# Channel LayerNorm of a convolution branch: cross-partition sums by a matrix of ones against transposes with tokens on partitions, with a weight split moved into the same stage

## The chip, the cores and the metric

The kernel runs on one core of a Trainium2 chip. The metric is the time of one execution on the device in microseconds (us); lower is better. Kernels are compared by the median of several runs.

## The reference

Two request groups (512 and 1024 tokens, width 1024) go through a two-layer encoder with the same weights. In the kernel they are one array of 1536 rows (12 tiles of 128 tokens). The part that matters here is layer 0's mixer:

```python
def conv_branch(u, gate, w, b, g, beta):
    h = u * jax.nn.sigmoid(gate)
    h = depthwise_conv_width_31(h, w) + b            # per channel, along the tokens
    return jax.nn.silu(layer_norm(h, g, beta))       # mean and variance over the 512 channels

conv_out = conv_branch(u, gate, conv_w, conv_b, cln_g, cln_b)
attn_out = window_attention(q, k, v, sink)
mix = jnp.concatenate([conv_out, attn_out], axis=-1) @ w_out     # 1024 -> 1024
x = layer_norm(ALPHA * x + mix, ln1_g[layer], ln1_b[layer])      # then the router and the experts
```

`layer_norm` subtracts the mean over the channels, multiplies by 1/sqrt(variance + 1e-5), then by a gain and adds a shift per channel. All is float32. The products with `w_out` are made of three passes on numbers rounded for the fast matmul path: high x high, high x low, low x high, where low is what high leaves of the number.

## The kernel before, in words

`trunk` calls one function per stage. Every stage opens with `Core.stage()`: it takes its own buffers and semaphores, holds one block of instruction streams (one per engine, in written order), and ends with a barrier of all engines (L129). So work of different stages never overlaps, and what one stage ends later starts all that follow later.

The stages around the change, in layer 0:

`window_and_taps` (its last instructions end at 503 us of the span) leaves the convolution's result in `cat[:, 0:4, :]`: channels on partitions (4 tiles of 128 channels), 1536 tokens along the row. `cat[:, 4:8, :]` holds the attention's output in the same layout. During it SP also loads the raw output weights, 8 pieces `early[k]` of 128 x 1024.

`norm_channels` (L639) normalises over channels, which here lie across partitions. It works in three chunks of 512 tokens. PE multiplies a 128 x 128 matrix of 1/512 with the 4 channel tiles (L685): each partition of `mean_ps` then holds the mean of each token. DVE subtracts it in place (L672), ACT squares 4 x 512 columns (L713), PE sums the squares in the same manner (L694), ACT takes the root (L715), DVE the reciprocal of 512 columns (L676) and multiplies (L679), ACT applies gain, shift and Silu from per-partition columns (L720). All three chunks of reciprocals and products stand behind the three subtractions in DVE's order.

`project_out` (L774) multiplies `cat` by the output weights, tile by tile of 128 tokens. It first splits the weights: ACT copies `early[k]` into `wh` (L991), DVE subtracts to get `wl` (L942), and PE waits for `w_low` piece by piece during tile 0's first half (`arriving`, L861 and following). Of each token tile ACT makes `ah` (L954), DVE `al` (L910), PE runs 48 matmuls of 512 columns (L864), DVE adds the residual (L917) and normalises the row (L162 to L173, with 1/sqrt by POOL's `pow`, L851), PE transposes it (L887) for the router. `ah`, `al` have two slots, `y_ps` two halves of PSUM.

`experts` and layer 1 follow, with barriers between them; `project_out` also serves layer 1, where 5 of 8 weight pieces are loaded in its own stage.

Of the kernel before, what the change touches and what calls it, by code (L numbers as in the profile page):

```python
# [14 lines left out]
P = 128  # L15
D = 1024
KD = D // P
# [621 lines left out]
def norm_channels(c, m, acc, cat):  # L639
    nc = c.nc  # L640
    with c.stage():
        par = c.sb("conv_par", [P, 2, CT])
        ones = c.sb("ones", [P, P])
        eps = c.sb("eps", [P, 1])
        sq = c.sb("sq", [P, 2, CT, HALF])
        rstd = c.sb("rstd", [P, TOK // HALF, HALF])
        mean_ps, var_ps = c.ps("mean_ps", TOK), c.ps("var_ps", HALF)
        loaded, dve, const = c.sem("loaded"), c.sem("dve"), c.sem("const")
        mean_done, centred, squared, var_done, rooted, normed, cat_done = (
            c.sem(n) for n in ("mean_done", "centred", "squared", "var_done", "rooted", "normed", "cat_done"))  # L650
        chunks = TOK // HALF
        with c.block() as block:

            @block.sync
            def _(sp):
                for n, name in enumerate(("conv_g", "conv_beta")):
                    sp.dma_start(par[:, n, :], m[name]).then_inc(loaded, 16)

            @block.gpsimd
            def _(pool):  # L660
                pool.memset(ones[:], 1.0 / CONV).then_inc(const, 1)
                pool.memset(eps[:], LN_EPS).then_inc(const, 1)

            @block.vector
            def _(v):
                s = Steps(v, dve)
                v.wait_ge(loaded, 32)
                for n in range(chunks):
                    part = acc[:, :, n * HALF:(n + 1) * HALF]
                    v.wait_ge(mean_done, n + 1)  # L670
                    for ct in range(CT):
                        nc.vector.tensor_tensor(part[:, ct, :], part[:, ct, :], mean_ps[:, n * HALF:(n + 1) * HALF], ALU.subtract).then_inc(centred, 1)  # L672
                for n in range(chunks):
                    part = acc[:, :, n * HALF:(n + 1) * HALF]
                    v.wait_ge(rooted, n + 1)
                    s.link(nc.vector.reciprocal(rstd[:, n, :], rstd[:, n, :]))  # L676
                    v.wait_ge(centred, CT * (n + 1))
                    for ct in range(CT):
                        nc.vector.tensor_tensor(part[:, ct, :], part[:, ct, :], rstd[:, n, :], ALU.mult).then_inc(normed, 1)  # L679

            @block.tensor
            def _(pe):
                def mean(n):
                    for ct in range(CT):
                        last = nc.tensor.matmul(mean_ps[:, n * HALF:(n + 1) * HALF], ones[:], acc[:, ct, n * HALF:(n + 1) * HALF],  # L685
                                                start=(ct == 0), stop=(ct == CT - 1))
                    last.then_inc(mean_done, 1)

                def variance(n):
                    pe.wait_ge(squared, n + 1)  # L690
                    if n:
                        pe.wait_ge(rooted, n)
                    for ct in range(CT):
                        last = nc.tensor.matmul(var_ps[:], ones[:], sq[:, n % 2, ct, :], start=(ct == 0), stop=(ct == CT - 1))  # L694
                    last.then_inc(var_done, 1)

                pe.wait_ge(const, 1)
                mean(0)
                for n in range(chunks):
                    if n + 1 < chunks:  # L700
                        mean(n + 1)
                    variance(n)

            @block.scalar
            def _(act):
                act.wait_ge(const, 2)
                act.wait_ge(loaded, 32)
                for n in range(chunks):
                    part = acc[:, :, n * HALF:(n + 1) * HALF]
                    act.wait_ge(centred, CT * (n + 1))  # L710
                    if n >= 2:
                        act.wait_ge(var_done, n - 1)
                    nc.scalar.activation(sq[:, n % 2], part, ACT.Square).then_inc(squared, 1)  # L713
                    act.wait_ge(var_done, n + 1)
                    nc.scalar.activation(rstd[:, n, :], var_ps[:], ACT.Sqrt, bias=eps[:]).then_inc(rooted, 1)  # L715
                for n in range(chunks):
                    part = acc[:, :, n * HALF:(n + 1) * HALF]
                    act.wait_ge(normed, CT * (n + 1))
                    for ct in range(CT):
                        nc.scalar.activation(cat[:, ct, n * HALF:(n + 1) * HALF], part[:, ct, :], ACT.Silu,  # L720
                                             bias=par[:, 1, ct:ct + 1], scale=par[:, 0, ct:ct + 1]).then_inc(cat_done, 1)
# [1256 lines left out]
```

## Time and profile before

| | us |
|---|---|
| median of 3 runs | 3780.56 |
| lowest, highest | 3777.04, 3785.15 |
| profiled execution, its own time | 3778.59 |
| its span, first to last instruction | 3776.7 |
| PE busy | 3390.5 (90%) |
| DVE busy | 2564.3 (68%) |
| ACT busy | 2022.3 (54%) |
| POOL busy | 343.9 (9%) |
| mean granted TensorE clock | 0.955 of full |

How to read it: the busy times are averages over stages with different limits. Since the stages are cut apart by barriers, what an edit in one of them is worth is read between that stage's first and last instruction. In rows of the timeline the columns are start us, duration us of the merged group, engine, line, operation, out<-in, shape, count, and in brackets the engine's idle time before it with what released it. PEld is the load of the stationary operand, an engine name with q (SPq) a queue that issues DMAs. The granted clock in the windows view is a share of 2.4 GHz: 0.50 is 1.2 GHz.

### The profile page before, as it was taken

What the parts mean: (1) busy time and instruction counts of PE and PEld (TensorE: products, weight loads), DVE (VectorE), ACT (ScalarE), POOL (GpSimd) and SP (SyncE); (2) the same over time, 40 slices, a digit from 0 to 9 for tenths busy, and PEclk for the clock granted to TensorE, in tenths of its full rate; (3) what the DMA queues carried; (4) which work ended last, traced back from release to release, by engine and by line L of the source; (5) the groups of instructions that cost most, each with busy time, mean ns of one, the idle gap of its engine ahead of it and who ended that gap; (6) DMA issues with size and microseconds to landing.
All of it is one profiled execution on the core that took longest, in us unless ns stands there. A gap on an engine that the chain in (4) does not pass through costs nothing. (4 is left out here: it accounts for less than half of the span.)

```text
span 3776.7 us, 51640 instructions
## 1 busy us (share of the span) xinstructions
PE 3390.5 (90%) x18712; PEld 2729.4 (72%) x18712; DVE 2564.3 (68%) x3959; ACT 2022.3 (54%) x2797; POOL 343.9 (9%) x302
## 2 busy tenths in 40 slices
PE   9986669699999999988996899998959999999993
PEld 7873338589999999973453455666859999999992
DVE  3688975766766767644664778885676766766765
ACT  3116752256665666641334877883236666666654
POOL 0000000010110111101110000000011111110102
PEclk9998889799999999998998999999979999999996
DMA  3101203477777778734211110003267777877774
GB/s 123 37 29 35 65 30 117 150 240 248 246 246 257 237 246 257 235 108 154 82 78 57 39 34 22 22 17 110 110 210 238 255 250 240 255 249 245 248 225 153
DMA packets 359950, 585.50 MB, mean 155 GB/s; under 512 B 17440, under 2 KB 283680, under 8 KB 358304
## 3 DMA queue, kind: packets, MB, share of 16 engines
q1 hardware_dynamic: 335136, 489.67, 38.4%
q0 software_dynamic: 14336, 50.34, 6.0%
q10 hardware_dynamic: 10368, 44.04, 2.9%
q8 instruction: 67, 1.10, 0.1%
q14 instruction: 43, 0.35, 0.0%
HBM read 505.36 MB, written 78.64 MB: 155 GB/s over the span
## 5 line engine op out<-in xcount | busy, mean ns | idle before, releaser
L1186 PE MATMUL h_ps<-xT,high 128*128 128x384 f32 x3584 | 1063.8, 359 | 2.7 <-DVE xT L1308 2.7
L1304 DVE TENSOR_TENSOR low<-raw,high 128x2048 fp32r<-128x2048 f32 x384 | 877.0, 2285 | 154.9 <-ACT high L1248 148.0
L1187 PE MATMUL h_ps<-xT,low 128*128 128x192 f32 x3584 | 904.4, 252 | 0.0
L1248 ACT ACTIVATE high<-raw 128x2048 fp32r<-128x2048 f32 x384 | 733.1, 1910 | 284.9 <-PE yp_ps L1219 176.2
L1187 PEld LDWEIGHTS h_ps<-xT,low 128*128 128x128 f32 x3584 | 683.3, 191 | 1.3
L1186 PEld LDWEIGHTS h_ps<-xT,high 128*128 128x128 f32 x3584 | 674.3, 188 | 5.0 <-issue 3.5
L1364 DVE TENSOR_TENSOR gate_up<-h_ps,cross 128x384 f32<-128x384 f32 x256 | 142.8, 558 | 306.5 <-ACT cross L1267 306.5
L1267 ACT ACTIVATE cross<-h_ps 128x384 f32<-128x384 f32 x256 | 125.6, 491 | 278.8 <-PE h_ps L1190 278.7
L1500 PE MATMUL qkv_ps<-w_in,xT 128*128 128x512 f32 x576 | 255.8, 601 | 8.4 <-ACT xT L1520 6.9
L1760 DVE TENSOR_REDUCE col<-s_ps 128x1 f32<-128x1024 f32 (+1 forms) x192 | 200.5, 1044 | 77.9 <-PE s_ps L1715 77.1
L200 DVE SCALAR_TENSOR_TENSOR cat<-glu,taps,cat 128x264 f32<-128x264 f32 (+28 forms) x412 | 248.0, 671 | 0.0
L1797 ACT ACTIVATE p<-s_ps,col 128x1024 f32<-128x1024 f32 (+1 forms) x192 | 186.5, 971 | 59.2 <-DVE col L1760 59.2
L1802 ACT ACTIVATE p<-p,col 128x1024 f32<-128x1024 f32 (+1 forms) x192 | 193.5, 1008 | 44.2 <-DVE col L1764 44.2
L1715 PE MATMUL s_ps<-keys,q 128*128 128x512 f32 x640 | 200.1, 427 | 13.8 <-DMA q<-rows_qT_parts 11.4
L1715 PEld LDWEIGHTS s_ps<-keys,q 128*128 128x128 f32 x640 | 106.4, 190 | 146.0 <-issue 130.0
L1500 PEld LDWEIGHTS qkv_ps<-w_in,xT 128*128 128x128 f32 x576 | 108.5, 192 | 141.6 <-issue 127.7
L1209 PE MATMUL y_ps<-high,hT 128*128 128x512 f32 x512 | 203.8, 398 | 0.0
L1210 PE MATMUL y_ps<-low,hT 128*128 128x512 f32 x512 | 203.4, 397 | 0.0
L1219 PE MATMUL yp_ps<-low,hT 128*64 128x512 f32 x512 | 202.0, 394 | 0.0
L1215 PE MATMUL yp_ps<-high,hT 128*128 128x512 f32 x512 | 201.9, 394 | 0.0
L1208 PE MATMUL y_ps<-high,hT 128*128 128x512 f32 x512 | 201.4, 393 | 0.0
L1771 DVE COPY pT<-t_ps 128x1024 f32<-128x1024 f32 (+1 forms) x192 | 199.0, 1036 | 3.4 <-PE t_ps L1723 3.4
(240 smaller groups left out, 5813.3 us busy)
## 6 DMA issues: line engine op xcount, KB each, us to landing
raw<-moe_w_gate SPq DMA_DIRECT2D x128, 1024.0 KB, 5.4
raw<-moe_w_up SPq DMA_DIRECT2D x128, 1024.0 KB, 7.9
raw<-moe_w_down SPq DMA_DIRECT2D x128, 1024.0 KB, 6.8
rows_x<-x ACTq DMA_DIRECT2D x36, 512.0 KB, 2.7
rows_acc<-ax ACTq DMA_DIRECT2D x24, 512.0 KB, 2.8
r<-rows_acc SPq DMA_DIRECT2D x24, 512.0 KB, 8.0
rows_qT_parts<-qT ACTq DMA_DIRECT2D x12, 1024.0 KB, 3.9
q<-rows_qT_parts SPq DMA_DIRECT2D x24, 512.0 KB, 3.6
```

What stands on the lines that cost most here:

```text
L200: return nc.vector.scalar_tensor_tensor(conv[:, one, lo:hi], glu[:, one, lo + step:hi + step], weight, conv[:, one, lo:hi], ALU.mult, ALU.add)
L1186: nc.tensor.matmul(ps, wh[:, n, k, :], xT[:, u, k, :, :].rearrange("p s n -> p (s n)"), start=(k == 0), stop=False)
L1187: nc.tensor.matmul(ps[:, 0:SLOTS], wl[:, n, k, :], xT[:, u, k, 0, :], start=False, stop=False)
L1208: nc.tensor.matmul(y_ps[:, cols], hT[:, f, 0:SC], wh[:, j, cols], start=first, stop=False)
L1209: nc.tensor.matmul(y_ps[:, cols], hT[:, f, SC + 2 * PC:2 * SLOTS], wh[:, j, cols], start=False, stop=False)
L1210: nc.tensor.matmul(y_ps[:, cols], hT[:, f, 0:SC], wl[:, j, cols], start=False, stop=end)
L1215: return nc.tensor.matmul(yp_ps[:, cols], hT[:, f, SC:SC + 2 * PC], wh[:, j, cols], start=first, stop=end)
L1219: return nc.tensor.matmul(yp_ps[0:PC, cols], hT[:, f, SC:SLOTS], wl[:, j, cols], start=False, stop=False)
L1248: nc.scalar.activation(split_view(high, at), piece_view(at), ACT.Copy).then_inc(high_ready, 1)
L1304: nc.vector.tensor_tensor(split_view(low, at), piece_view(at), split_view(high, at).bitcast(F32), ALU.subtract).then_inc(low_ready, 1)
L1500: last = nc.tensor.matmul(qkv_ps[:, n * HALF:(n + 1) * HALF], xT[:, k * P:(k + 1) * P], w[:, k, n * HALF:(n + 1) * HALF], start=(k == 0), ...
L1715: last = nc.tensor.matmul(s_ps[n % 2][:, b * HALF:(b + 1) * HALF], q[:, side, n * P:(n + 1) * P], keys[:, 2 * (2 * side + n // SHARE) + pa ...
```

## The change: what it does

`norm_channels` is written anew. It works on 12 tiles of 128 tokens. For each, PE transposes 4 blocks of 128 x 128 of `cat` into `f_ps[t % 2]` (tokens on partitions, 512 channels along the row), DVE takes mean and variance with `bn_stats` and `bn_aggr`, POOL raises variance + eps to -0.5, DVE makes -mean times that, ACT writes (value * rstd + bias) to `row[:, t % 2]`, PE transposes 4 blocks back into `b_ps`, and for each pair of tiles ACT applies Silu with gain and shift per channel and writes `cat`. In the same stage ACT and DVE split the 8 pieces of output weights; `project_out` for layer 0 gets `wh` and `wl` finished, no longer waits for `w_low`, and starts with `high`/`low` of its first token tile. `spare` and `wh` are allocated ahead of both stages. Layer 1 keeps the old path.

In the diff a line "..." stands for removed lines of `norm_channels`, which are printed above.

```diff
@@ -636,89 +636,129 @@
                 out(TILES - 1)
-def norm_channels(c, m, acc, cat):
+def norm_channels(c, m, cat, early, wh, wl):
+
     nc = c.nc
+    PAIRS = TILES // 2
     with c.stage():
         par = c.sb("conv_par", [P, 2, CT])
...
+        ident, half = c.sb("ident", [P, P]), c.sb("minus_half", [P, 1])
+        stats, mv = c.sb("stats", [P, 2, 6]), c.sb("mv", [P, 2, 5])
+        row = c.sb("row", [P, 2, CONV])
+        f_ps, b_ps = [c.ps("f_ps0", CONV), c.ps("f_ps1", CONV)], [c.ps("b_ps0", CT * 2 * P), c.ps("b_ps1", CT * 2 * P)]
+        ident_in, par_in, const, dve = c.sem("ident_in"), c.sem("par_in"), c.sem("const"), c.sem("dve")
+        turned, var_ready, rstd_ready, bias_ready, normed, returned, cat_ready = (
+            c.sem(n) for n in ("turned", "var_ready", "rstd_ready", "bias_ready", "normed", "returned", "cat_ready"))
+        w_high, w_low = c.sem("w_high"), c.sem("w_low")
+
+        def as_raw(k, view):
+            return view.rearrange("p (j n) -> p j n", n=early[k].shape[2])
+
         with c.block() as block:
             @block.sync
             def _(sp):
+                sp.dma_start(ident[:], m["ident"]).then_inc(ident_in, 16)
                 for n, name in enumerate(("conv_g", "conv_beta")):
...
+                    sp.dma_start(par[:, n, :], m[name]).then_inc(par_in, 16)
             @block.gpsimd
             def _(pool):
...
+                pool.memset(half[:], -0.5).then_inc(const, 1)
+                pool.wait_ge(const, 1)
+                for t in range(TILES):
+                    pool.wait_ge(var_ready, t + 1)
+                    pool.tensor_tensor(mv[:, t % 2, 3:4], mv[:, t % 2, 2:3], half[:], ALU.pow).then_inc(rstd_ready, 1)
+
+            @block.tensor
+            def _(pe):
+                def turn(t):
+                    if t >= 2:
+                        pe.wait_ge(normed, t - 1)
+                    for ct in range(CT):
+                        last = nc.tensor.transpose(f_ps[t % 2][:, ct * P:(ct + 1) * P], cat[:, ct, t * P:(t + 1) * P], ident[:])
+                    last.then_inc(turned, 1)
+
+                def turn_back(t):
+                    pair, side = t // 2, t % 2
+                    pe.wait_ge(normed, t + 1)
+                    if pair >= 2:
+                        pe.wait_ge(cat_ready, pair - 1)
+                    for ct in range(CT):
+                        at = ct * 2 * P + side * P
+                        last = nc.tensor.transpose(b_ps[pair % 2][:, at:at + P], row[:, side, ct * P:(ct + 1) * P], ident[:])
+                    last.then_inc(returned, 1)
+
+                pe.wait_ge(ident_in, 16)
+                turn(0)
+                turn(1)
+                for t in range(TILES):
+                    turn_back(t)
+                    if t + 2 < TILES:
+                        turn(t + 2)
             @block.vector
             def _(v):
                 s = Steps(v, dve)
...
+
+                def measure(t):
+                    of = mv[:, t % 2, :]
+                    v.wait_ge(turned, t + 1)
+                    if t >= 2:
+                        v.wait_ge(normed, t - 1)
+                    s.link(nc.vector.bn_stats(stats[:, t % 2, :], f_ps[t % 2][:]))
+                    s.link(nc.vector.bn_aggr(of[:, 0:2], stats[:, t % 2, :]))
+                    nc.vector.tensor_scalar(of[:, 2:3], of[:, 1:2], LN_EPS, None, ALU.add).then_inc(var_ready, 1)
+
+                def shift(t):
+                    of = mv[:, t % 2, :]
+                    v.wait_ge(rstd_ready, t + 1)
+                    nc.vector.scalar_tensor_tensor(of[:, 4:5], of[:, 0:1], -1.0, of[:, 3:4], ALU.mult, ALU.mult).then_inc(bias_ready, 1)
+
+                def low(k):
+                    v.wait_ge(w_high, k + 1)
+                    nc.vector.tensor_tensor(as_raw(k, wl[:, k, :]), early[k], as_raw(k, wh[:, k, :]).bitcast(F32), ALU.subtract).then_inc(w_low, 1)
+
+                measure(0)
+                for t in range(TILES):
+                    if t + 1 < TILES:
+                        measure(t + 1)
+                    shift(t)
+                    if t >= TILES - KD:
+                        low(t - (TILES - KD))
+                v.wait_ge(w_low, KD)
             @block.scalar
             def _(act):
...
+                def normalise(t):
+                    of = mv[:, t % 2, :]
+                    act.wait_ge(bias_ready, t + 1)
+                    if t >= 2:
+                        act.wait_ge(returned, t - 1)
+                    nc.scalar.activation(row[:, t % 2, :], f_ps[t % 2][:], ACT.Identity, bias=of[:, 4:5], scale=of[:, 3:4]).then_inc(normed, 1)
+
+                def silu(pair):
+                    act.wait_ge(returned, 2 * pair + 2)
                     for ct in range(CT):
...
+                        last = nc.scalar.activation(cat[:, ct, pair * 2 * P:(pair + 1) * 2 * P], b_ps[pair % 2][:, ct * 2 * P:(ct + 1) * 2 * P], ACT.Silu,
+                                                    bias=par[:, 1, ct:ct + 1], scale=par[:, 0, ct:ct + 1])
+                    last.then_inc(cat_ready, 1)
+
+                def high(k):
+                    nc.scalar.activation(as_raw(k, wh[:, k, :]), early[k], ACT.Copy).then_inc(w_high, 1)
+
+                high(0)
+                high(1)
+                for t in range(TILES):
+                    normalise(t)
+                    if t < KD - 2:
+                        high(t + 2)
+                    if t == 0:
+                        act.wait_ge(par_in, 32)
+                    if t >= 3 and t % 2:
+                        silu((t - 3) // 2)
+                silu(PAIRS - 1)
+                act.wait_ge(cat_ready, PAIRS)
@@ -771,13 +811,14 @@
             steps.settle()
-def project_out(c, m, layer, early, x_src, cat, picks, spare):
+def project_out(c, m, layer, early, x_src, cat, picks, spare, wh=None):
     nc = c.nc
     with c.stage():
-        EARLY = len(early)
+        EARLY, SPLIT = len(early), wh is not None
         raw = c.sb("w_raw", [P, 2, D]) if EARLY < KD else None
-        wh = c.sb("w_high", [P, KD, D], F32R)
+        if not SPLIT:
+            wh = c.sb("w_high", [P, KD, D], F32R)
         wl = spare[:, 0:KD * D].rearrange("p (k n) -> p k n", k=KD)
         wr = c.sb("router", [P, KD, EXPERTS])
         ident = c.sb("ident", [P, P])
@@ -869,7 +910,7 @@
                 def step(at, product, following, normed, routed):
                     before, old = at.next(-1), at.next(-2)
                     if product:
-                        products(at, 0, not normed)
+                        products(at, 0, not normed and not SPLIT)
                     if routed:
                         pe.wait_ge(xT_ready, old.t + 1)
                         pe.wait_ge(prob_ready, old.t + 1)
@@ -935,13 +976,16 @@
                 v.sem_inc(res_done, 2)
                 v.sem_inc(prob_ready, 1)
-                for k in range(KD):
-                    v.wait_ge(w_high, k + 1)
-                    if k and EARLY:
-                        v.wait_ge(w_low, k)
-                    nc.vector.tensor_tensor(as_raw(k, wl[:, k, :]), raw_weight(k), as_raw(k, wh[:, k, :]).bitcast(F32), ALU.subtract).then_inc(w_low, 1)
-                    if k == 0:
-                        low(Tile(0, 0))
+                if SPLIT:
+                    low(Tile(0, 0))
+                else:
+                    for k in range(KD):
+                        v.wait_ge(w_high, k + 1)
+                        if k and EARLY:
+                            v.wait_ge(w_low, k)
+                        nc.vector.tensor_tensor(as_raw(k, wl[:, k, :]), raw_weight(k), as_raw(k, wh[:, k, :]).bitcast(F32), ALU.subtract).then_inc(w_low, 1)
+                        if k == 0:
+                            low(Tile(0, 0))
                 picks.clear(nc, s).then_inc(blank, 1)
                 v.wait_ge(tables_in, 64)
                 steps_of(step)
@@ -985,12 +1029,15 @@
                 act.sem_inc(rT_done, 1)
                 for u in range(2):
                     act.sem_inc(x1_out[u], 32)
-                for k in range(KD):
-                    if k >= EARLY:
-                        act.wait_ge(w_in[k], 32)
-                    nc.scalar.activation(as_raw(k, wh[:, k, :]), raw_weight(k), ACT.Copy).then_inc(w_high, 1)
-                    if k == 0:
-                        high(Tile(0, 0))
+                if SPLIT:
+                    high(Tile(0, 0))
+                else:
+                    for k in range(KD):
+                        if k >= EARLY:
+                            act.wait_ge(w_in[k], 32)
+                        nc.scalar.activation(as_raw(k, wh[:, k, :]), raw_weight(k), ACT.Copy).then_inc(w_high, 1)
+                        if k == 0:
+                            high(Tile(0, 0))
                 steps_of(step)
                 for u in range(2):
                     act.wait_ge(x1_out[u], 32 * (TILES // 2) + 32)
@@ -1913,9 +1960,10 @@
                 weights = nc.alloc_sbuf_tensor_at("early_weights", [P, KD, 2, HALF], F32, offset=under_weights)
                 early = [weights[:, k, :, :] for k in range(KD)]
                 window_and_taps(c, m, keys, values, glu, cat, taps, conv_b, early)
-                norm_channels(c, m, cat[:, 0:CT, :], cat)
-            spare = c.sb("spare", [P, (KD + 4) * D], F32R)
-            project_out(c, m, 0, early, m["x"], cat, picks, spare[:])
+            spare, wh = c.sb("spare", [P, (KD + 4) * D], F32R), c.sb("w_high", [P, KD, D], F32R)
+            wl = spare[:, 0:KD * D].rearrange("p (k n) -> p k n", k=KD)
+            norm_channels(c, m, cat, early, wh, wl)
+            project_out(c, m, 0, early, m["x"], cat, picks, spare[:], wh)
         experts(c, m, 0, picks)
         with c.stage():
             under_keys = nc.alloc_sbuf_tensor_at("under_keys", [P, 2 * AX_KV, TOK], F32, offset=next_address(nc))
```

## Rows read from the trace of the kernel before

**Rows 1.** Busy time of each engine, its share of the span, instructions (the page).
```profile
PE 3390.5 (90%) x18712; PEld 2729.4 (72%) x18712; DVE 2564.3 (68%) x3959; ACT 2022.3 (54%) x2797; POOL 343.9 (9%) x302
```

**Rows 2.** Timeline of the channel normalisation's stage.
```profile
503.41 0.34 SPq L657 DMA_DIRECT2D conv_par<-conv_g  x1
...
519.23 2.48 DVE L672 TENSOR_TENSOR cat<-cat,mean_ps 128x512 f32<-128x512 f32 x4 [5.90 <-PE mean_ps L685]
...
533.21 3.35 DVE L676 RECIPROCAL rstd<-rstd 128x512 f32<-128x512 f32 x1
...
539.12 2.93 ACT L720 ACTIVATE cat<-cat,conv_par 128x512 f32<-128x512 f32 x4 [2.44 <-DVE cat L679]
```

**Rows 3.** Timeline of the start of the output projection, up to its second tile.
```profile
542.76 0.33 SPq L828 DMA_DIRECT2D x<-x  x1
...
543.27 1.06 ACT L991 ACTIVATE w_high<-early_weights 128x1024 fp32r<-128x1024 f32 x1 [1.22 <-PEq L129]
...
546.63 9.20 DVE L942 TENSOR_TENSOR spare<-early_weights,w_high 128x1024 fp32r<-128x1024 f32 x7
546.77 0.79 PE L864 MATMUL y_ps<-w_high,spare 128*128 128x512 f32 x1 [17.87 <-DVE spare L910]
...
562.34 1.22 DVE L917 SCALAR_TENSOR_TENSOR row<-x,y_ps 128x1024 f32<-128x1024 f32 x1 [4.49 <-PE y_ps L864]
...
573.23 1.22 DVE L917 SCALAR_TENSOR_TENSOR row<-x,y_ps 128x1024 f32<-128x1024 f32 x1 [2.77 <-PE y_ps L864]
```

**Rows 4.** Timeline of PE: eight transposes at the start of layer 1's projection, and later.
```profile
1713.32 1.94 PE L1477 MATMUL xT_ps<-ident,x 128*128 128x128 f32 x8 [32.51 <-DVE x L173]
...
1742.33 1.04 PE L1477 MATMUL xT_ps<-ident,x 128*128 128x128 f32 x8
```

**Rows 5.** Timeline of DVE and POOL in a row normalisation.
```profile
1713.09 1.28 DVE L162 BATCH_NORM_STATS2 stats<-r 128x6 f32<-128x512 f32 x2
...
1714.41 0.20 DVE L166 BATCH_NORM_AGGREGATE mv<-stats 128x2 f32<-128x12 f32 x1
...
1714.65 0.15 DVE L167 TENSOR_SCALAR mv<-mv 128x1 f32<-128x1 f32 x1
1714.88 0.55 POOL L1458 TENSOR_TENSOR mv<-mv,minus_half 128x1 f32<-128x1 f32 x1 [5.08 <-DVE mv L167]
```

**Rows 6.** Groups by form: count, busy us, mean ns of one, idle before and releaser.
```profile
L377 ACT ACTIVATE sig<-ug_ps 128x512 f32<-128x512 f32 x12 | 7.2, 598 | 115.5 <-PE ug_ps L304 115.5
L715 ACT ACTIVATE rstd<-var_ps,eps 128x512 f32<-128x512 f32 x3 | 2.1, 689 | 10.7 <-PE var_ps L694 10.7
L1538 ACT ACTIVATE parts<-qk 128x256 fp32r<-128x256 f32 x12 | 4.8, 399 | 0.0
L720 ACT ACT_TABLE_LOAD x1 | 1.3, 1283 | 0.0
```

**Rows 7.** DMA issues of the first 600 us: count, KB each, median us to landing.
```profile
ident<-ident SPq DMA_DIRECT2D x3, 64.0 KB, 1.8
```

**Rows 8.** Windows: length, busy (count) of PE, PEld, DVE, ACT, POOL; granted clock; DMA.
```profile
475.70:478.70 3.00, 0.00 (x0) 0.00 (x0) 2.48 (x7) 2.56 (x8) 0.00 (x0) 1.00 0.00 0
478.80:480.00 1.20, 1.20 (x11) 1.20 (x12) 1.20 (x7) 0.41 (x1) 0.00 (x0) 1.00 0.00 0
480.00:483.40 3.40, 3.40 (x17) 1.56 (x17) 3.33 (x9) 2.89 (x6) 0.00 (x0) 0.50 0.00 0
...
531.20:546.70 15.50, 0.00 (x0) 0.00 (x0) 10.20 (x12) 11.85 (x16) 0.10 (x1) 0.50 0.17 49
546.80:551.60 4.80, 4.80 (x11) 3.53 (x12) 4.48 (x4) 4.80 (x6) 0.00 (x0) 0.50 0.92 284
...
762.40:766.60 4.20, 3.88 (x16) 2.97 (x16) 2.80 (x4) 1.48 (x3) 0.00 (x0) 0.50 0.87 252
766.80:767.90 1.10, 0.00 (x0) 0.00 (x0) 0.65 (x2) 0.36 (x1) 0.00 (x0) 1.00 0.96 294
1713.30:1722.50 9.20, 8.07 (x16) 4.09 (x17) 4.69 (x8) 1.02 (x1) 0.55 (x1) 0.50 1.02 420
```

More of the change, by code:

```diff
@@ L636, in _ @@
                 out(TILES - 1)
-def norm_channels(c, m, acc, cat):
+def norm_channels(c, m, cat, early, wh, wl):
     nc = c.nc
+    PAIRS = TILES // 2
     with c.stage():
         par = c.sb("conv_par", [P, 2, CT])
[L643 to L651, printed above, removed]
+        ident, half = c.sb("ident", [P, P]), c.sb("minus_half", [P, 1])
[8 more added lines that the diff above has]
+            return view.rearrange("p (j n) -> p j n", n=early[k].shape[2])
         with c.block() as block:
@@ L655, in _ @@
             def _(sp):
+                sp.dma_start(ident[:], m["ident"]).then_inc(ident_in, 16)
                 for n, name in enumerate(("conv_g", "conv_beta")):
-                    sp.dma_start(par[:, n, :], m[name]).then_inc(loaded, 16)
+                    sp.dma_start(par[:, n, :], m[name]).then_inc(par_in, 16)
             @block.gpsimd
             def _(pool):
-                pool.memset(ones[:], 1.0 / CONV).then_inc(const, 1)
-                pool.memset(eps[:], LN_EPS).then_inc(const, 1)
+                pool.memset(half[:], -0.5).then_inc(const, 1)
[27 more added lines that the diff above has]
+                        turn(t + 2)
             @block.vector
@@ L666, in _ @@
                 s = Steps(v, dve)
[L667 to L702, printed above, removed]
+                def measure(t):
[6 more added lines that the diff above has]
+                    nc.vector.tensor_scalar(of[:, 2:3], of[:, 1:2], LN_EPS, None, ALU.add).then_inc(var_ready, 1)
@@ L704, in _ @@
+                for t in range(TILES):
[5 more added lines that the diff above has]
+                v.wait_ge(w_low, KD)
             @block.scalar
             def _(act):
[L706 to L715, printed above, removed]
@@ L716, in _ @@
-                for n in range(chunks):
-                    part = acc[:, :, n * HALF:(n + 1) * HALF]
-                    act.wait_ge(normed, CT * (n + 1))
-                    for ct in range(CT):
-                        nc.scalar.activation(cat[:, ct, n * HALF:(n + 1) * HALF], part[:, ct, :], ACT.Silu,
-                                             bias=par[:, 1, ct:ct + 1], scale=par[:, 0, ct:ct + 1]).then_inc(cat_done, 1)
+                def normalise(t):
[4 more added lines that the diff above has]
+                    nc.scalar.activation(row[:, t % 2, :], f_ps[t % 2][:], ACT.Identity, bias=of[:, 4:5], scale=of[:, 3:4]).then_inc(normed, 1)
```

## The prediction

> **What bounds the kernel now.** I read the page's busy shares first, then the timeline of the two stages that the change touches, then the windows for the granted clock. PE is busy 90% of the span [rows 1], but a share over the whole run says nothing of one stage, and stages are cut apart by barriers. So the change is worth what the end of the normalisation moves, plus what the start of the output projection moves.
>
> The normalisation's stage runs from SP's first issue at 503.41 to the end of the last Silu at 539.12 + 2.93 = 542.05: 38.64 us. It is a chain handed between DVE, ACT and PE: DVE waits 5.90 for the third mean, then holds the stage with a 3.35 us reciprocal and a product per chunk, then ACT closes [rows 2]. The projection begins at 542.76, its first matmul at 546.77, tile 0's residual at 562.34, tile 1's at 573.23 [rows 3]. From tile 1 on PE is the bound: 10.89 us for 48 matmuls, 0.227 each. Tile 0 takes 562.34 - 546.77 = 15.57, since it waits for the weight split (7 subtractions in 9.20) and starts at half clock [rows 3, 8].
>
> **The new stage.** Its shape is a ring. DVE's order is measure(t+1), shift(t), measure(t+2), shift(t+1). measure(t+2) waits for turn(t+2), which PE runs behind turn_back(t), which waits for normalise(t), which waits for shift(t). So two PSUM buffers don't give two tiles in flight: shift(t+1), whose inputs are long ready, stands in DVE's queue behind measure(t+2). Once round this ring is one tile. The terms:
> - shift: a one-column DVE instruction, 0.15 [rows 5], 0.16 taken.
> - normalise: 512 columns from PSUM take 598 ns without a per-partition operand and 689 with one; with two 0.78 [rows 6].
> - PE: 4 transposes back and 4 of the next tile, one run of 8. Eight took 1.94 at one clock level and 1.04 at the other [rows 4].
> - measure: 0.67 (half of 1.28 is 0.64; a single one is a little longer), 0.20 and 0.15 with about 0.05 between dependent ones: 1.13 [rows 5]. POOL's 0.55 lies off the ring, since it works on t+1 while the ring runs through tile t.
> - three handoffs at about 0.045 (1713.32 + 1.94 to the next user, 0.03; DVE to POOL 0.08) : 0.14.
>
> Sum 4.15 at 1.2 GHz, 3.25 at 2.4.
>
> **Which clock.** It falls behind gaps: after a pause of 3 us at full clock, PE ran 1.2 us of transposes and then stood at 0.50 (475.7 to 483.4) [rows 8]. It comes back only behind nearly unbroken work: 4.8 us of matmuls at 0.50 after the barrier, 16 transposes with 3.88 of 4.20 us busy, and in layer 1 not before 1722.5, although PE was busy 1.94 us from 1713.32 and 8.07 of 9.20 in all [rows 4, 8]. In the new stage PE works 1.94 of each 4.15 us, or 1.04 of 3.25. I take 1.2 GHz from the second tile on, and take 1.0 us off for the first, which may still run at full clock.
>
> The Trainium skill ("TensorE: Matmul & The Clock Gate", Part 4: PE-mode transpose) says that transposes don't count as busy for the clock. The rows of 762.4 to 767.9 speak against it: there the clock rose behind transposes alone. Here both lead to 1.2 GHz. The same page (Why this matters for your kernels) says that idle gaps below about 3 us don't cost the clock; the new gaps are 2.2 us, so by it the clock would stay at 2.4 GHz. The rows of 475.7 to 483.4 are at its edge. It is rival A.
>
> **The stage's sum.** Identity by SP issued at 503.41 lands 1.8 later [rows 7], ahead of everything PE does: 505.2. The first two turns are 1.04 together; measure(0) follows the first, measure(1) directly behind it, shift(0), normalise(0): 505.3 + 0.6 + 2 x 1.13 + 0.16 + 0.78 + handoffs = 509.3. ACT's high(0) and high(1) lie before that. Ten rounds end with normalise(10): 41.5. Beside the ring ACT has, per tile, a weight piece (1.06, [rows 3]) for t = 0 to 5 and per pair four Silus of 256 columns. One of these without per-partition operand is 399 [rows 6]; with two, 0.57, and back to back about 0.48: 2.0 for four. After normalise ACT is free for 3.37 of a round. Only t = 3 breaks that: 1.0 + 1.28 table load [rows 6] + 2.0 = 4.3, a delay of 0.9. DVE's low (1.23 to 1.31, [rows 3]) fits into its wait of 2.9 per round, free for six of eight. So normalise(10) ends at 509.3 + 41.5 + 0.9 - 1.0 = 550.7. For tile 11 the low(6) queued between shift(10) and shift(11) is on the path: normalise(11) ends at 550.7 - 0.8 + 1.23 + 0.16 + 0.8 = 552.1. Then two Silu groups, 2 x 2.0, as turn_back(11) is ready at 553.2: the stage ends at 556.1, 14.1 us later than now.
>
> Removed on the way: the matmuls with ones, the squares, both table loads but one, three reciprocals; all are inside the 38.64 that go. The weight split moves in at no cost but the 1.23 above. Its ACT part would cost up to 8 x 1.06 if ACT bound the stage; it has 2.4 of spare per round without it.
>
> **The projection.** Barrier and issue gap are as before, 0.71 to SP's issue. First matmul: 0.51 until ACT starts, high 1.05, low 1.2, handoffs 0.1 = 2.9 instead of 4.01 [rows 3]: 1.1 saved. Tile 0: PE starts at half clock again, since it was idle for 3 us and more. 4.9 us at 0.43 each are 11.5 matmuls, the other 36.5 at 0.227 are 8.3: 13.2 instead of 15.57, 2.3 saved; bounds 10.9 (full clock at once, 4.7 saved) and 15.0 (half clock for 8 us). Its tables land some 9 us after the stage's start and DVE waits for them before low(1), which PE needs at 16: no wait. From tile 1 on PE binds as before, so the gain is kept.
>
> Sum: 14.1 - 1.1 - 2.3 = +10.7 us. Against the profiled execution's own 3778.59 that is 3789.3. The median of the runs lies 2.0 above it: 3780.56 + 10.7 = 3791.3. I forecast 3791.
>
> The bounds of what isn't in the trace: each handoff 0.03 to 0.15 (ring 4.1 to 4.5, ten rounds: -0.5 to +3); normalise 0.69 to 0.85 (-1 to +0.7); Silus 0.4 to 0.6 each, eight at the end (-0.7 to +1); ident 1.7 to 3.6; the clock, as in rival A.
>
> **Rivals.**
> A. The clock stays at 2.4 GHz through the new stage. The ring is 3.25, ten rounds 32.5. ACT at t = 3 and 5 then delays by 1.8 and 0.5, so normalise(10) ends at 509.3 + 32.5 + 2.3 = 544.1 and the stage at 549.5, +7.4; less 1.1 and 2.3, as PE still idles at least 6 us around the barrier: +4.0, 3784.6. For it: gaps of 2.2 us only. Against: the fall at 480, behind a pause of 3 us and 1.2 us of transposes [rows 8], a pattern close to the new one, and it would have to hold twelve times. A clock that changes back and forth gives about 3788. Together 0.2.
>
> B. The handoffs dominate more than I count, 0.15 for each of three in the ring plus more between dependent one-column instructions: 4.65 per round, +5: 3796. For it: seven dependent steps per tile; against: rows 5, where they stand 0.05 apart. 0.1.
>
> C, on the other side: the tiles do overlap, and the stage is bound by its busiest engine and not by the ring. ACT's work is 12 x 0.78 + 8 x 0.96 + 1.28 + 6 x 2.0 = 30.3; behind a head of 2 us and a tail of 2 the stage ends at 538, 4 earlier than now, and with 1.1 and 2.3 saved the kernel takes 3773. For it: two buffers of each kind, and no engine is full. Against: DVE's written order, which the engine can't leave. It decides at 3.1 us per tile: below that the change gains. 0.05.
>
> D. The split in the stage doesn't hide, or the projection's head gains nothing, since PE's cold start takes what the missing waits give: the first 15.57 stay as they are, +13: 3794. For it: 4.9 us of half clock are in tile 0 either way, and its waits cost only 0.36 per piece after the rise. Against: at half clock too the pieces came no faster than every 1.3 us. 0.1.
>
> The forecast itself 0.55.
>
> **How the numbers follow.** What a measurement of this kernel can tell from no change is 0.2%, 7.6 us: 3773.0 to 3788.1. The forecast's own range is 3787 to 3796, mostly above that line. Slower by over 0.2%: 0.55 x 0.85 + B 0.1 + D 0.1 + a part of A, 0.03 = 0.70. Within: 0.08 from the forecast, 0.17 from A, 0.01 = 0.26. Faster: 0.04. The range is 3783 to 3797: it takes in A, B and D and leaves C and half of the tails out.
>
> **What would show it.** Right: in the new stage the normalising activations start 4.1 to 4.2 apart, DVE's idle time stands before bn_stats and is released by PE, windows show the clock at 0.50 from about the second tile, the last Silu ends near 556; the projection's first matmul comes 2.9 behind its stage's first issue, tile 0 takes about 13.2, tile 1 still 10.9; everything behind is shifted by one amount. Wrong: rounds of 3.2 (A), 4.6 (B), bn_stats released by nothing with ACT without idle time (C), or a shift behind the projection that isn't the sum of the two stages.

## The result and the profile after

The changed kernel takes 3792.13 us (median of 6 runs, 3787.60 to 3796.68) against 3780.26 of before: ratio 1.0032, 95% interval 1.0019 to 1.0045. It is slower by 11.9 us; the forecast was 3791. The profiled execution took 3787.60, 9.0 more than the profiled one of before (3778.59).

The stages show where. The timeline of DVE in the new normalisation, two rounds of the ring and the end (columns as in the rows of before):

```profile
511.70 0.70 DVE L709 BATCH_NORM_STATS2 stats<-f_ps 128x6 f32<-128x512 f32 x1 [2.94 <-PE f_ps L679]
...
512.72 0.15 DVE L716 SCALAR_TENSOR_TENSOR mv<-mv 128x1 f32<-128x1 f32 x1
515.74 0.70 DVE L709 BATCH_NORM_STATS2 stats<-f_ps 128x6 f32<-128x512 f32 x1 [2.87 <-PE f_ps L679]
...
545.94 1.22 DVE L720 TENSOR_TENSOR spare<-early_weights,w_high 128x1024 fp32r<-128x1024 f32 x1
547.60 0.16 DVE L716 SCALAR_TENSOR_TENSOR mv<-mv 128x1 f32<-128x1 f32 x1 [0.44 <-POOL mv L671]
...
554.72 1.23 DVE L951 TENSOR_TENSOR spare<-cat,spare 128x1024 fp32r<-128x1024 f32 x1 [5.83 <-ACT spare L998]
...
569.44 1.22 DVE L958 SCALAR_TENSOR_TENSOR row<-x,y_ps 128x1024 f32<-128x1024 f32 x1 [6.71 <-PE y_ps L905]
```

ACT and PE over the same round, then ACT's last Silus:

```profile
512.91 0.78 ACT L738 ACTIVATE row<-f_ps,mv 128x512 f32<-128x512 f32 x1 [2.32 <-DVE mv L716]
...
518.69 1.28 ACT L743 ACT_TABLE_LOAD   x1
519.99 1.93 ACT L743 ACTIVATE cat<-b_ps,conv_par 128x256 f32<-128x256 f32 x4
521.80 0.79 ACT L738 ACTIVATE row<-f_ps,mv 128x512 f32<-128x512 f32 x1
...
548.47 3.74 ACT L743 ACTIVATE cat<-b_ps,conv_par 128x256 f32<-128x256 f32 x8
```
```profile
501.85 1.19 PE L679 MATMUL f_ps<-ident,cat 128*128 128x128 f32 x8 [3.23 <-DMA ident<-ident]
...
513.74 1.11 PE L689 MATMUL b_ps<-ident,row 128*128 128x128 f32 x4 [2.07 <-ACT row L738]
514.64 1.06 PE L679 MATMUL f_ps<-ident,cat 128*128 128x128 f32 x4
...
556.00 0.80 PE L905 MATMUL y_ps<-w_high,spare 128*128 128x512 f32 x1 [6.26 <-DVE spare L951]
```

Read in a circle (measure, shift, normalise and turning back are the functions of the change): shift ends at 512.87, normalise runs 512.91 to 513.69, PE turns back and ahead from 513.74 until 515.70, and DVE measures at 515.74. One round is 515.74 - 511.70 = 4.04. Each engine waits for the one before it: DVE 2.87, PE 2.07, ACT 2.32, all in the same 4.04. The t = 3 round has the table load in it, as forecast, and takes 4.86 (519.78 to 524.64).

The last row of interest is 547.60: shift(11) waits 0.44 for POOL, which the forecast held to be off the path. SP, POOL and the windows:

```profile
500.03 0.34 SPq L661 DMA_DIRECT2D ident<-ident  x1
...
553.13 0.33 SPq L869 DMA_DIRECT2D x<-x  x1
```
```profile
516.93 0.55 POOL L671 TENSOR_TENSOR mv<-mv,minus_half 128x1 f32<-128x1 f32 x1 [3.49 <-DVE mv L711]
520.97 1.53 POOL L671 TENSOR_TENSOR mv<-mv,minus_half 128x1 f32<-128x1 f32 x1 [3.49 <-DVE mv L711]
```
```profile
500.00:502.80 2.80, 0.95 (x8) 0.86 (x8) 0.26 (x1) 2.00 (x2) 0.10 (x1) 0.98 0.13 25
503.00:516.00 13.00, 5.95 (x25) 4.70 (x24) 4.04 (x16) 5.17 (x6) 2.20 (x4) 0.50 0.00 0
516.00:550.00 34.00, 16.01 (x64) 12.41 (x64) 17.79 (x41) 19.82 (x33) 11.25 (x8) 0.50 0.00 0
550.00:556.00 6.00, 0.00 (x0) 0.00 (x0) 1.28 (x2) 4.22 (x7) 0.10 (x1) 0.50 0.30 98
556.00:560.60 4.60, 4.60 (x11) 3.63 (x12) 0.71 (x3) 0.00 (x0) 0.00 (x0) 0.50 0.95 277
560.70:569.40 8.70, 8.70 (x39) 7.17 (x39) 1.22 (x1) 0.00 (x0) 0.00 (x0) 1.00 0.11 40
```

In the windows the figure behind POOL's is the granted clock: full until about 502.7, then 0.50 (1.2 GHz) through the whole stage and for the first 4.7 us of the projection.

From the profiled execution of each kernel, in us. "Stage" goes from SP's first issue in it to the end of the last Silu, "head" from SP's first issue in the projection to its first matmul, "tile 0" from there to the residual of tile 0, and the last column adds all, with the gap between the stages:

| | stage | head | tile 0 | stage's start to tile 0's residual |
|---|---|---|---|---|
| before [rows 2, 3] | 38.64 | 4.01 | 15.57 | 58.93 |
| changed | 52.18 | 2.87 | 13.44 | 69.41 |
| forecast | 52.7 | 2.9 | 13.2 | 69.5 |

Tile 1 takes 10.89 in both. So 10.5 of the 11.9 us lie here. The rest lies outside the two stages, where both kernels run the same code. Ahead of them the profiled executions differ by 3.4 us the other way: this stage begins at 503.41 before and at 500.03 in the changed kernel. Behind tile 0 the changed kernel takes 2.0 us longer, 3216.4 against 3214.4, and 1.7 of that is one event in the first expert of layer 0: TensorE goes back to 2.4 GHz 35.5 us behind the expert stage's first issue before (766.8, [rows 8]), and 40.9 us behind it in the changed kernel:

```profile
767.90:774.50 6.60, 3.91 (x16) 3.14 (x16) 5.04 (x6) 1.96 (x4) 1.66 (x1) 0.50 0.87 241
774.80:778.50 3.70, 3.67 (x13) 3.68 (x14) 0.00 (x0) 0.00 (x0) 0.00 (x0) 0.50 0.81 322
779.30:781.00 1.70, 1.70 (x14) 1.70 (x13) 0.00 (x0) 0.00 (x0) 0.00 (x0) 1.00 0.00 0
```

In the seven experiments below it takes 39.7 to 41.3 us, and that stage 968.0 to 969.4 us against 966.7 before. There is one profile of before, so whether its early rise is chance isn't shown. The single executions of either kernel differ by 8 to 9 us in all. That is why the experiments are judged by this table first and by their medians second; but a row of it is one execution, and it says what the two stages take, not what the kernel gains.

### The profile page after: what moved, and what is told of

It reads as the page before. It is cut to its first block and busy times, and to the rows that moved or that the text cites. A ratio compares the mean times of both kernels' runs of the same rounds, so it can differ in the third digit from the quotient of the medians.

```text
span 3785.8 us, 51793 instructions
## 1 busy us (share of the span) xinstructions
PE 3388.7 (90%) x18760; PEld 2738.0 (72%) x18760; DVE 2551.5 (67%) x3980; ACT 2024.3 (53%) x2814; POOL 362.9 (10%) x313
## 5 line engine op out<-in xcount | busy, mean ns | idle before, releaser
L1762 PE MATMUL s_ps<-keys,q 128*128 128x512 f32 x640 | 199.8, 426 | 13.8 <-DMA q<-rows_qT_parts 11.3
```

What stands on the lines that cost most here:

```text
L1762: last = nc.tensor.matmul(s_ps[n % 2][:, b * HALF:(b + 1) * HALF], q[:, side, n * P:(n + 1) * P], keys[:, 2 * (2 * side + n // SHARE) + pa ...
```

## The experiments

**The new normalisation without the moved split, and the moved split without the new normalisation.** The changed kernel with the split back in the projection:

```diff
-                high(0)
-                high(1)
...
-                    if t < KD - 2:
-                        high(t + 2)
...
-                    if t >= TILES - KD:
-                        low(t - (TILES - KD))
-                v.wait_ge(w_low, KD)
...
-            project_out(c, m, 0, early, m["x"], cat, picks, spare[:], wh)
+            project_out(c, m, 0, early, m["x"], cat, picks, spare[:], wh, False)   # wh allocated outside, split inside
```

> The changed kernel with the weight split put back into the projection, only the transposing normalisation left. My account: rounds still 4.04; the table load no longer delays a round (0.85 less), tile 11 isn't behind a subtraction (0.8 less), so the stage takes 50.5 to 51; POOL's pow stays at 0.55 throughout instead of 1.53; the projection is as before (4.0 and 15.5): 12 more than before, 3792. Rival (the split on ACT and DVE is what makes the stage long): stage below 45, kernel at 3785 or less.

Measured: 3793.79, ratio to before 1.0033 (1.0021 to 1.0045). Stage 50.47, head 4.01, tile 0 15.59, and rounds of 4.04 throughout. POOL's pow next to no subtraction:

```profile
546.89 0.55 POOL L671 TENSOR_TENSOR mv<-mv,minus_half 128x1 f32<-128x1 f32 x1 [3.49 <-DVE mv L711]
```

The other half, the old normalisation with the split in its stage:

```diff
+                for k in range(6):          # ACT, ahead of the first square; 6 and 7 behind it
+                    high(k)
...
+                low(0)                      # DVE, ahead of the first mean
+                low(1)
...
+                    if n == 1:              # while it waits for the third mean
+                        for k in range(2, 6):
+                            low(k)
...
+                low(6)                      # behind the last product, beside the last Silus
+                low(7)
```

> The changed kernel with the old normalisation (ones matmuls, three chunks) put back, and the weight split kept in its stage: ACT's first six pieces while it has nothing else, two behind the first square; DVE's in its idle time and two behind its last product. My account (the ring of the new normalisation costs 13.5 us, the moved split saves 1.1 and 2.1 in the projection): the stage stays at 38.6 to 39.5 us, the projection's first matmul comes 2.9 behind its first issue, tile 0 takes 13.4; the kernel takes 3.3 less than before, 3777. Rival (the moved split gains nothing, since PE's half clock at the projection's start eats it): 3780, tile 0 still 15.5.

Measured: 3779.94 against 3781.28, ratio 0.9995 (0.9986 to 1.0004): by time alone no verdict. The 3777 that I expected wasn't reached, and the median is the rival's number, so the stage's rows have to decide. It takes 38.65, head 3.16, tile 0 13.65, 56.18 in all, 2.75 less than before. DVE in the stretch where it used to wait 5.90 [rows 2]:

```profile
507.93 2.48 DVE L683 TENSOR_TENSOR cat<-cat,mean_ps 128x512 f32<-128x512 f32 x4 [0.88 <-PE mean_ps L701]
510.32 4.63 DVE L674 TENSOR_TENSOR spare<-early_weights,w_high 128x1024 fp32r<-128x1024 f32 x4
516.31 2.48 DVE L683 TENSOR_TENSOR cat<-cat,mean_ps 128x512 f32<-128x512 f32 x4 [1.36 <-PE mean_ps L701]
```

Four subtractions lie in a wait, and the third centring comes as late as it did. So the two halves of the change have opposite signs: the new normalisation costs 50.47 - 38.64 = 11.8 without the split, the split saves about 2.8 where it hides, and in the changed kernel it takes 52.18 - 50.47 = 1.7 of that back, in the round of the table load (0.8) and at tile 11 (1.0). Both rivals fall by the rows: the split isn't what makes the stage long, and tile 0 took 13.65 and not 15.5, so PE's half clock doesn't eat its gain. That the 2.8 us arrive in the kernel's own time isn't shown.

**What makes the ring: DVE's order.** The changed kernel with one thing moved:

```diff
-                measure(0)
                 for t in range(TILES):
-                    if t + 1 < TILES:
-                        measure(t + 1)
+                    measure(t)
                     shift(t)
```

> The changed kernel with DVE's order measure(0), shift(0), measure(1), shift(1), ... instead of measure(t+1), shift(t). Each shift now waits 0.7 for POOL, but isn't queued behind a measure that waits for PE. My account (the stage is bound by the written order, not by an engine): two tiles in flight, about 2.5 per tile until the subtractions begin and 3.1 with them; stage about 41, 11 less than changed; kernel 3781. Rival (half clock on PE or ACT's work is the bound): rounds stay at 4, kernel within 2 of 3792.

Measured: 3778.54 against 3781.28, ratio 0.9991 (0.9982 to 1.0001): 13.6 less than the changed kernel, and no verdict against before. The stage takes 40.27, 11.9 less than changed, with every instruction of the changed kernel still there.

```profile
528.94 0.69 DVE L709 BATCH_NORM_STATS2 stats<-f_ps 128x6 f32<-128x512 f32 x1
529.67 0.18 DVE L710 BATCH_NORM_AGGREGATE mv<-stats 128x2 f32<-128x6 f32 x1
529.88 0.15 DVE L711 TENSOR_SCALAR mv<-mv 128x1 f32<-128x1 f32 x1
530.70 0.16 DVE L716 SCALAR_TENSOR_TENSOR mv<-mv 128x1 f32<-128x1 f32 x1 [0.66 <-POOL mv L671]
530.77 1.22 DVE L720 TENSOR_TENSOR spare<-early_weights,w_high 128x1024 fp32r<-128x1024 f32 x1
531.91 0.69 DVE L709 BATCH_NORM_STATS2 stats<-f_ps 128x6 f32<-128x512 f32 x1
```

From tile 7 on bn_stats has no wait before it any more (tiles 2, 4 and 6 still waited 0.7 to 1.0 for PE); DVE waits only 0.66 for POOL, and a tile takes 531.91 - 528.94 = 2.97, all of it DVE's own instructions and that wait. The order measure(t+1), shift(t) was there to hide POOL's 0.66, and put 2.87 behind PE in its place.

**The clock in the ring.** Sixteen extra transposes of the identity in PE's pause, per tile:

```diff
                     if t + 2 < TILES:
                         turn(t + 2)
+                    if t < TILES - 1:
+                        for j in range(16):
+                            nc.tensor.transpose(x_ps[:, j % 4 * P:(j % 4 + 1) * P], ident[:], ident[:])
```

> The changed kernel with 16 transposes of the identity (128 x 128, into a PSUM bank of their own) behind each tile's work in PE's pause. If transposes keep the clock at 2.4 GHz, as the trace before suggests: 16 take 1.84 and fit the pause, PE's eight take 1.03, rounds 3.1 to 3.2, stage about 43, kernel 3783. Rival (transposes don't count for the clock, as a page has it): 16 take 3.4, which is 1.4 more than the pause, rounds 5.4 and more, stage about 66, kernel 3806.

Measured: 3789.69, ratio 1.0019 (1.0010 to 1.0028). Stage 46.28. Windows and PE's timeline:

```profile
508.60:514.90 6.30, 4.76 (x23) 4.76 (x24) 1.71 (x8) 3.20 (x4) 1.40 (x3) 0.50 0.00 0
515.00:527.00 12.00, 9.32 (x82) 8.61 (x81) 4.44 (x13) 8.25 (x12) 2.62 (x3) 1.00 0.01 1
527.00:549.00 22.00, 19.16 (x164) 17.50 (x162) 14.72 (x32) 13.68 (x26) 9.18 (x6) 1.00 0.01 1
```
```profile
511.91 3.40 PE L702 MATMUL x_ps<-ident 128*128 128x128 f32 x16
...
518.25 0.66 PE L690 MATMUL b_ps<-ident,row 128*128 128x128 f32 x4 [0.33 <-ACT row L742]
518.75 0.60 PE L680 MATMUL f_ps<-ident,cat 128*128 128x128 f32 x4
519.18 1.91 PE L702 MATMUL x_ps<-ident 128*128 128x128 f32 x16
521.42 0.66 PE L690 MATMUL b_ps<-ident,row 128*128 128x128 f32 x4 [0.33 <-ACT row L742]
```

More work on PE makes the stage 5.9 shorter. The clock rises at about 515 behind transposes alone, which PE had run without a pause from 510.14, and stays at 2.4 GHz to the stage's end; a round is then 521.42 - 518.25 = 3.17, 0.87 less than at 1.2 GHz. The sum is less than ten times that, since the first rounds still ran at half clock and ACT's t = 3 round (4.86) doesn't get shorter. Against the Trainium skill ("TensorE: Matmul & The Clock Gate", Part 4: PE-mode transpose), by which transposes don't count as busy, the measurement decides: here they lifted the clock by themselves. The run also gives rival A its price: with 2.4 GHz from the third tile on, the stages take 63.44 - 58.93 = 4.5 more than before (rival A had 4.0) and the median is 8.4 above before's, so the change would have been slower even so.

Whether gaps as short as the ring's keep the clock, as rival A has it, the change itself doesn't test: PE had waited 3.23 for the identity, and the clock fell 0.9 behind the first transposes, ahead of the gaps of 2.07. The run with the shift moved does:

```profile
524.40:527.20 2.80, 1.26 (x10) 0.86 (x8) 2.24 (x5) 1.58 (x4) 0.38 (x2) 1.00 0.01 3
527.20:527.70 0.50, 0.00 (x0) 0.00 (x0) 0.00 (x0) 0.00 (x0) 0.49 (x1) 1.00 0.00 0
527.80:528.70 0.90, 0.00 (x0) 0.00 (x0) 0.90 (x2) 0.78 (x2) 0.00 (x0) 0.50 0.00 0
```

There PE was at 2.4 GHz, waited 1.47 (until 526.04), worked 1.09, and was at 1.2 GHz from about 527.75, 0.6 into a wait of 1.62. In the spread run further down it kept 2.4 GHz through a wait of 1.82 (527.46 to 529.28). So waits shorter than the ring's didn't always keep the clock, and their length alone doesn't say whether it falls.

**What makes the ring: the buffers.** DVE's order as in the change, four buffers in place of two:

```diff
-        f_ps = [c.ps("f_ps0", CONV), c.ps("f_ps1", CONV)]
+        f_ps = [c.ps(f"f_ps{u}", CONV) for u in range(4)]     # and stats, mv: [t % 4]
...
-                    if t >= 2:
-                        pe.wait_ge(normed, t - 1)
+                    if t >= 4:
+                        pe.wait_ge(normed, t - 3)
...
-                    if t + 2 < TILES:
-                        turn(t + 2)
+                    if t + 4 < TILES:
+                        turn(t + 4)
```

> The changed kernel with DVE's order left as it is, but four buffers for the turned tile, its statistics and its scale instead of two, and PE turning four tiles ahead. My account (the ring closes through the two buffers and the order): measure(t+2) no longer waits for normalise(t), the stage is bound by ACT's work, 31 to 33, kernel 3772. Rival (the order alone makes the ring, buffers don't help): rounds stay at 4.04 and the kernel at 3792.

Measured: 3772.73 against 3780.14, ratio 0.9979 (0.9970 to 0.9989). The stage takes 31.86, 20.3 less than in the change and 6.8 less than before. ACT is the bound now, with 21.95 of 23 us busy in this window:

```profile
507.00:530.00 23.00, 14.58 (x76) 13.23 (x76) 18.71 (x52) 21.95 (x34) 12.93 (x11) 0.70 0.00 1
```

So the ring needs both, the order and the two buffers (of the turned tile, its statistics and its scale; `row` keeps two here); undoing either breaks it. Rival C of the prediction had a stage bound by its busiest engine at 538 - 503.4 = 34.6; this edit gets there and 2.7 below.

**A version that beats both.** Four buffers, four of ACT's weight pieces ahead of tile 0, the subtractions from tile 1 on, each Silu group one tile earlier:

```diff
+                for k in range(4):
+                    high(k)
...
+                    if t < KD - 4:
+                        high(t + 4)
...
+                    if 1 <= t <= KD:
+                        low(t - 1)
...
+                    if t >= 2 and t % 2 == 0:
+                        silu((t - 2) // 2)
```

> Four buffers as in the run before, four of ACT's weight pieces ahead of the first tile instead of two, the subtractions from tile 1 on instead of tile 4, and each pair's Silu one tile earlier. ACT is the bound: about 1.5 for two pieces moved into its first wait and 1.9 for one Silu group less behind the last tile, against 1.2 of turning back that now shows: stage 29 to 31, kernel 3769 to 3771, 0.3% less than before. Rival (PE's half clock binds once the tiles overlap, 1.94 each and waits between): stage 33 or more, kernel 3773.

Measured: 3773.52, ratio 0.9979 (0.9970 to 0.9988): no better than the run before, and both expectations are missed. The stage is 31.47, not 29 to 31. A Silu group that comes one tile earlier waits for PE to turn back a tile that has only just been normalised, here tile 5 and tile 11 in ACT's timeline:

```profile
523.28 1.93 ACT L743 ACTIVATE cat<-b_ps,conv_par 128x256 f32<-128x256 f32 x4 [0.54 <-PE b_ps L689]
...
533.79 1.93 ACT L743 ACTIVATE cat<-b_ps,conv_par 128x256 f32<-128x256 f32 x4 [1.21 <-PE b_ps L689]
```

Last, the same with PE put to work at the projection's start:

```diff
+                if SPLIT:
+                    for j in range(5):
+                        nc.tensor.matmul(t_ps[:, 0:HALF], wh[:, j, 0:P], wh[:, j, 0:HALF], start=True, stop=True)
```

> The run before, and five more matmuls of 512 columns on the finished weights at the very start of the projection, into a PSUM tile that is not used yet, while ACT and DVE split the first token tile. If tile 0's 13.4 against 10.9 is PE's half clock, which ends some 4.9 us after PE begins, these take up to 2.1 of it in dead time: tile 0 at 11.3 to 12.5, kernel 1 to 2 less than the run before. Rival (the half clock lasts until the real products have run for a while, or the first matmul is pushed back by the extra ones): tile 0 stays at 13.4.

Measured: 3769.70 against 3780.14, ratio 0.9974 (0.9963 to 0.9984), 22 us below the changed kernel's 3792.13. Head 2.87, tile 0 12.64 instead of 13.56, just outside what was expected (11.3 to 12.5). The rows give 1.3 us less than the run before; the 3.8 between the two medians isn't resolved, as their intervals overlap.

```profile
533.70 2.47 PE L912 MATMUL t_ps<-w_high 128*128 128x512 f32 x5 [2.93 <-PEq L129]
536.51 0.80 PE L905 MATMUL y_ps<-w_high,spare 128*128 128x512 f32 x1 [0.34 <-DVE spare L955]
```

The extra matmuls take 2.47 of dead time and the first product isn't later. Part of the half clock is now ahead of the real products, which gains 0.9 and not 2.1: how much one gains differs from execution to execution, as the rise came 5.8 us behind PE's first matmul here and 4.7 in the changed kernel. The runs taken together show that tile 0's excess over 10.9 is the clock. In the seven profiles with the split moved, tile 0 spends between 3.0 and 5.5 us at 1.2 GHz (last column below, from windows of 0.5 us), and its length is 10.9 + 0.36 + 0.47 for each of these us, within 0.1. The 0.47 is 1 - 0.227/0.43, the share lost at the longer pitch, and 0.36 lies at the two ends of the tile (the next section says where).

| | us (median) | ratio to before | stage | head | tile 0 | sum | tile 0 at 1.2 GHz |
|---|---|---|---|---|---|---|---|
| changed | 3792.13 | 1.0032 | 52.18 | 2.87 | 13.44 | 69.41 | 4.7 |
| no split in it | 3793.79 | 1.0033 | 50.47 | 4.01 | 15.59 | 70.98 | 6.1 |
| old normalisation, split in it | 3779.94 | 0.9995 | 38.65 | 3.16 | 13.65 | 56.18 | 5.2 |
| shift behind measure | 3778.54 | 0.9991 | 40.27 | 2.88 | 12.92 | 56.98 | 3.6 |
| extra transposes | 3789.69 | 1.0019 | 46.28 | 2.88 | 13.37 | 63.44 | 4.6 |
| four buffers | 3772.73 | 0.9979 | 31.86 | 2.87 | 13.79 | 49.55 | 5.5 |
| four buffers, spread | 3773.52 | 0.9979 | 31.47 | 2.88 | 13.56 | 48.82 | 5.0 |
| and warm start | 3769.70 | 0.9974 | 31.07 | 2.87 | 12.64 | 47.49 | 3.0 |

The sum holds the gap between the stages, and is 58.93 before. From "shift behind measure" down, the sums differ from before's by -2.0, +4.5, -9.4, -10.1 and -11.4 us, and the medians by -2.7, +8.4, -7.4, -6.6 and -10.4: up to 3.9 apart. Part of it is the layer 0 expert stage of above, which took 1.2 to 2.7 us more in all of them than in the one profile of before; the rest isn't located.

## Why the prediction was right, point by point

- The ring was right in its path and its size: 4.04 a round for 4.15. normalise took the 0.78 that was built from rows of one and no per-partition operand; bn_stats from PSUM 0.70 for 0.67. That it is the order with the two buffers is shown by the two runs that undo one of them.
- The clock was right for the stage, 1.2 GHz throughout. It fell earlier than I took: at about 502.7, ahead of the first normalise, so the 1.0 us that I took off for the first tile wasn't there. The ten rounds, 1.1 shorter together than forecast, hide that error.
- ACT's t = 3 round cost 0.82 for 0.9. The last two Silu groups took 3.74 for 4.0.
- "POOL's 0.55 lies off the ring" held for the ring, but not for tile 11: there POOL took 1.53 and shift(11) came 0.44 behind the subtraction that I had named as the only delay.
- Head 2.87 for 2.9, tile 0 13.44 for 13.2, although the half clock lasted 4.7 us instead of 4.9. By the two pitches that gives 13.1. PE's rows have the other 0.3 (and the bound of 15.0 for 8 us at half clock works out as 14.7): the second product starts 0.60 behind the first and not 0.43 (556.00, 556.60), and the residual follows the start of the last product (569.02) by 0.42 and not by a pitch of 0.227.
- The gap between the last Silu and the projection's first issue was taken as before, 0.71; it is 0.92 (552.21 to 553.13), and 0.91 in the runs without the split and with the shift moved, 0.72 with the old normalisation. Why isn't shown.
- The sum was +10.7; the rows give +10.5 (stage 13.5 for 14.1, gap 0.2 for nothing, head 1.1 saved, tile 0 2.1 saved for 2.3), the medians +11.9. So the mechanism is right and the sum close because its small errors offset each other; that 3791 lies 1.1 from the median is partly luck, as there is no term in it for the 1.4 beyond the rows.
- That "everything behind is shifted by one amount" wasn't so: layer 0's expert stage took 1.7 longer, with the clock's later rise. The row on which the argument on transposes rested, a rise behind sixteen of them in that stage (762.4 to 766.8), is the only one of its kind: in the eight other profiles the rise comes behind the matmuls after them, in the run with the old normalisation too, where the sixteen stand as close together. The run with extra transposes is what shows it.
- Rival A (full clock) was wrong on the fact and right on its sign. The run with the shift moved lost the clock behind waits of 1.47 and 1.62, shorter than the ring's 2.07. Rival D (no gain in the projection) and B (long handoffs) are refuted by the table and by the 0.04 to 0.05 between the rows of a round. Rival C didn't occur in the change, and the four-buffer run shows that it was the design that the change lacked.
- Not shown: why the stage starts up to 4.6 us apart in these executions (500.03 to 504.60) with the same code ahead of it, and whether the 1.4 us between the rows' difference and the medians' are the clock's rise in the experts (1.7 in the profiles).

## What to carry to other kernels

Two buffers don't put two tiles in flight if an engine's written order puts the step that releases tile t+1 behind a step that waits for tile t+2; walk once round the chain of waits and read the period from it before trusting the buffers. Moving a step into a stage is free only where the engine is idle there, and its gain and the gain of what it travels with have to be measured apart: here they had opposite signs. An engine that works in short bursts can be the place to add work, if its clock pays for it.

## What the runs showed of the hardware

- POOL's pow on one column took 0.55 us alone and 1.53 beside DVE's subtraction of 1024 columns (520.97, while DVE ran 520.87 to 522.09), in every such pair of the changed kernel, of the one with extra transposes and of those with four buffers. It took 0.55 in all twelve tiles of the two kernels where no subtraction ran beside it, and also beside bn_stats (503.80). DVE's own 1.22 didn't change.
- Transposes alone brought TensorE from 1.2 to 2.4 GHz (at 515 in the run with extra transposes, behind 4.8 us of them without a pause), and a stage that was entered at 1.2 GHz and had eight transposes in every 4.04 us never left it.
- At the projection's start the rise to 2.4 GHz came 3.6 to 5.5 us behind PE's first matmul in the six profiles that run the same products there in the same order; each us at 1.2 GHz cost tile 0 0.47.
- Eight transposes, four back and four ahead, took 1.96 at 1.2 GHz (513.74 to 515.70) and 1.10 at 2.4 (518.25 to 519.35), the one for the other worth 0.87 a round.
